# mLSTM layer on one core: stabiliser rows and state weights spread over the partitions by DMA instead of by TensorE

## What is computed

```python
log_d = where(causal, cum_f[t] - cum_f[s] + li[s], -inf)
log_inter = cum_f + m_st
m_t = maximum(log_inter, max(log_d, axis=-1))           # the stabiliser of each row
w_inter = exp(log_inter - m_t)                          # weight of the state in each row
scores = (q k^T) * exp(log_d - m_t)
num = w_inter * (q c_st) + scores v
den = w_inter * (q n_st) + sum(scores)
h = num / maximum(abs(den), exp(-m_t))
c_st = decay * c_st + (w_k k)^T v                       # and n_st, m_st likewise
```

## Time and profile before

| | us |
|---|---|
| median of three runs (2153.97 to 2157.39) | 2154.73 |
| the profiled execution | 2154.42 |
| its span | 2152.8 |
| TensorE busy | 2121.9 |
| VectorE busy | 1425.7 |
| ScalarE busy | 939.2 |
| GpSimd busy | 250.1 |

### The profile page before, as it was taken

One profiled execution on the slowest core, in us unless ns is written; L12 is line 12 of the kernel. 1 busy time (PEld: TensorE's weight loads), 2 busy tenths in 40 slices (PEclk: granted clock), 3 DMA queues, 4 the chain that ended last, 5 costly groups with the idle time before them and its releaser, 6 DMA issues.

```text
span 2152.8 us, 29471 instructions
## 1 busy us (share of the span) xinstructions
PE 2121.9 (99%) x10424; PEld 1762.6 (82%) x10440; DVE 1425.7 (66%) x2274; ACT 939.2 (44%) x1686; POOL 250.1 (12%) x357
## 2 busy tenths in 40 slices
PE   6999999999999999999999999999999999999999
PEld 5888888888888888888878888888888888888887
DVE  8765476787566565679677644767866657556764
ACT  5433674453333333345444347544533333334443
POOL 3211100021001010100121111001110101001000
PEclk9999999999999999999999999999999999999999
DMA  4333373223322334773414334632233232357443
GB/s 148 110 110 113 109 272 121 84 69 106 105 96 97 117 102 150 270 249 118 152 64 142 118 94 147 233 119 89 68 103 109 97 117 96 105 190 250 152 134 107
DMA packets 200288, 281.56 MB, mean 131 GB/s; under 512 B 12912, under 2 KB 131696, under 8 KB 200176
## 3 DMA queue, kind: packets, MB, share of 16 engines
q1 hardware_dynamic: 171696, 183.07, 26.5%
q0 software_dynamic: 28480, 97.02, 12.9%
HBM read 197.73 MB, written 82.31 MB: 130 GB/s over the span
## 4 chain that ended last, share of the span: by engine, by line
PE 94%; DVE 3%; DMA 1%; ACT 1%; issue 1%; POOL 0%; SPq 0%; DVEq 0%; POOLq 0%
PE ps L2247 13%; PE ps L2250 13%; PE ps L2249 13%; PE ps L1971 7%; PE ps L1975 7%; PE ps L1973 7%; PE ps L2295 6%; PE ps L2297 6%; PE ps L2299 6%; PE ps L1884 3%; PE ps L1886 3%; PE ps L1885 3%; PE ps L1891 2%; PE ps L2157 1%; DMA res<-in_x_dram 1%
## 5 line engine op out<-in xcount | busy, mean ns | idle before, releaser
L1722 DVE TENSOR_TENSOR ring<-raw_f,ring 128x512 fp32r<-128x512 f32 x308 | 211.4, 687 | 188.1 <-ACT ring L1148 186.6
L1148 ACT CAST ring<-raw_f 128x512 fp32r<-128x512 f32 x308 | 191.2, 623 | 208.7 <-PE ps L2250 193.2
L2247 PE MATMUL ps<-u_lo,ring 128*128 128x512 f32 x704 | 275.7, 392 | 0.0
L2250 PE MATMUL ps<-u_hi,ring 128*128 128x512 f32 x704 | 274.1, 389 | 0.0
L2249 PE MATMUL ps<-u_hi,ring 128*128 128x512 f32 x704 | 273.9, 389 | 0.0
L2295 PE MATMUL ps<-ring,ring 128*128 128x512 f32 x616 | 240.5, 390 | 2.0 <-DVE ring L1801 1.9
L2299 PE MATMUL ps<-ring,ring 128*128 128x512 f32 x616 | 239.7, 389 | 0.0
L2297 PE MATMUL ps<-ring,ring 128*128 128x512 f32 x616 | 239.7, 389 | 0.0
L2247 PE MATMUL ps<-t_op,ring 128*128 128x512 f32 x528 | 206.0, 390 | 0.0
L2250 PE MATMUL ps<-t_op,ring 128*128 128x512 f32 x528 | 205.5, 389 | 0.0
L2249 PE MATMUL ps<-t_op,ring 128*128 128x512 f32 x528 | 205.4, 389 | 0.0
(11 more groups left out here) (223 smaller groups left out, 4180.3 us busy)
## 6 DMA issues: line engine op xcount, KB each, us to landing
ops_hbm<-kept POOLq DMA_DIRECT2D x154, 256.0 KB, 2.4
g_in<-ops_hbm SPq DMA_DIRECT2D x154, 256.0 KB, 2.7
raw<-in_ml_w_in_dram SPq DMA_DIRECT2D x24, 1024.0 KB, 5.4
proj_hbm<-pkept POOLq DMA_DIRECT2D x96, 256.0 KB, 2.7
raw_f<-in_ffn_w_gate_dram SPq DMA_DIRECT2D x44, 512.0 KB, 4.7
raw_f<-in_ffn_w_up_dram SPq DMA_DIRECT2D x44, 512.0 KB, 4.6
b<-in_ffn_w_down_dram SPq DMA_DIRECT2D x88, 256.0 KB, 4.6
x_in<-in_x_dram SPq DMA_DIRECT2D x16, 512.0 KB, 6.3
```

What stands on the lines that cost most here:

```text
L1148: nc.scalar.copy(four(ring[slot][:, 0, :]), feed_source(q, s)).then_inc(w_hi_done, 1)
L1722: nc.vector.tensor_tensor(four(ring[slot][:, 1, :]), feed_source(q, s), four(ring[slot][:, 0, :].bitcast(F32)), ALU.subtract).then_inc(w_l ...
L2247: pe.matmul(banks(bank), wh, moved(kind, 1, k), start=(fresh and k == 0), stop=False, skip_group_check=True)
L2250: last = pe.matmul(banks(bank), wl, moved(kind, 0, k), start=False, stop=(k == 3), skip_group_check=True)
```

## The change

The rows are spread by DMA. Behind the gates GpSimd stores `t4` and `t2` to a new tensor in DRAM, `rows_hbm` (`store_rows`, behind the stores of projection groups 1 and 4). SP loads them back, for each chunk, with one row on many partitions: `negb` [128, 8 heads, 128] and `wq` [128, 4 pairs, 128], two buffers of each (`load_rows`). VectorE adds the causal mask to `negb` in SBUF (`mask_rows`), ScalarE takes its exponentials from `negb`, and VectorE its weights and the decay from `wq`. `spread`, the products of `weights` (now `turn_keys`, the key transposes alone), `negm`, `wint`, `pick`, `ident_b`, `dec` and their set-up go away. `state_sums` no longer waits for `qw_done` and `dec_done`; `outputs` waits for `qw_done`. `load_res(0)` moves ahead of the last store of the projections. "Orders" are a few moves of `op_hi` and `op_lo` (high and low parts of turned tiles) past neighbouring work on ScalarE and VectorE.

```diff
+                def load_rows(c):
+                    s = c % 2
+                    if c >= 2:
+                        sp.wait_ge(dmat_done, h * 64 + 8 * (c - 1))
+                        sp.wait_ge(qw_done, h * 8 + c - 1)
+                        sp.wait_ge(state_done, h * 32 + 4 * (c - 1))
+                    sp.dma_start(negb[s][:, :, :].rearrange("p i t -> p (i t)"),
+                                 rows_hbm[h, 0, c:c + 1, :].partition_broadcast(P)).then_inc(negb_loaded[s], 16)
+                    for a in range(2):
+                        rows = rows_hbm[h, 1, c, :].rearrange("(g a n) -> a g n", a=2, n=P)
+                        sp.dma_start(wq[s][64 * a:64 * a + 64, :, :], rows[a].partition_broadcast(64))\
+                            .then_inc(wq_loaded[s], 16)
...
                 load_qkc(2)
+                load_rows(2)
                 load_og(1)
                 load_wo(1, 0)
...
                 for c in range(3, TILES):
                     load_qkc(c)
+                    load_rows(c)
                     load_vtc(c)
                     load_og(c)
...
+                                pool.wait_ge(p_fed, h * PU + PU - 1)
+                                load_res(0)
                             pool.wait_ge(o_gated, done + 3 + i)
                             store_block(g, k)
...
+                    if g in (1, 4):
+                        store_rows(0 if g == 1 else 1)
...
-                        nc.scalar.activation(dmat[:, i, :], ps[:, spread_bank(c) + i // 4, (i % 4) * P:(i % 4) * P + P],
-                                             ACT.Exp, bias=colt[:, c, i:i + 1]).then_inc(dmat_done, 1)
+                        nc.scalar.activation(dmat[:, i, :], negb[c % 2][:, i, :], ACT.Exp, bias=colt[:, c, i:i + 1])\
+                            .then_inc(dmat_done, 1)
...
+                def mask_rows(c):
+                    dve.wait_ge(negb_loaded[c % 2], h * 64 + 16 * (c // 2) + 16)
+                    nc.vector.tensor_tensor(negb[c % 2][:, :, :], negb[c % 2][:, :, :],
+                                            mask[:, :].unsqueeze(1).broadcast_to([P, HEADS, P]), ALU.add)\
+                        .then_inc(darg_done, 1)
...
+                    if n == unit_at(PG - 1, 0):
+                        mask_rows(0)
+                    if n == unit_at(PG - 1, 2):
+                        mask_rows(1)
...
-                    nc.vector.tensor_copy(dec[:, :], banks(2).rearrange("p (g t) -> p g t", t=P)[:, :, P - 1])\
-                        .then_inc(dec_done, 1)
-                    nc.vector.tensor_tensor(qw[:, :, :], banks(2).rearrange("p (g t) -> p g t", t=P),
-                                            qkc[c % 2][:, 0:4, :], ALU.mult).then_inc(qw_done, 1)
+                    nc.vector.tensor_tensor(qw[:, :, :], wq[c % 2][:, :, :], qkc[c % 2][:, 0:4, :], ALU.mult)\
+                        .then_inc(qw_done, 1)
...
                         hg_low(c - 1)
+                        if c + 1 < TILES:
+                            mask_rows(c + 1)
                     update_state(c)
...
                     op_hi(0, 2)
+                    op_hi(0, 3)
                     norm1_sum(0, 4)
-                    op_hi(0, 3)
...
+                    op_lo(0, 4)
                     proj_lo(0, 3)
-                    op_lo(0, 4)
...
+                op_lo(st + 1, 5)
                 feed_low(0, 3)
-                op_lo(st + 1, 5)
...
-                        if TURN_AT <= e < TURN_AT + 4:
-                            op_lo(2 * (h + 1), e - TURN_AT)
                         if e in ROWS_AT:
                             norm1_rows(h + 1, ROWS_AT[e])
                         if e in SUMS_AT:
                             sum_early(2 * (h + 1), SUMS_AT[e])
+                        if TURN_AT <= e < TURN_AT + 4:
+                            op_lo(2 * (h + 1), e - TURN_AT)
```

More of the change, by code:

```diff
@@ L723, in _ @@
                 pool.wait_ge(turned, st * OP_UNITS + OP_UNITS)
-                for tile in (cols[:, :], negm[:, :].bitcast(F32), wint[:, :].bitcast(F32)):
-                    nc.gpsimd.memset(tile, 0.0).then_inc(prep_done, 1)
+                nc.gpsimd.memset(cols[:, :], 0.0).then_inc(prep_done, 1)
                 def store_block(g, k):
@@ L888, in gate_part @@
                             .then_inc(gate_act, 1)
-                        nc.scalar.copy(negm[0:HEADS, now], t4[:, :]).then_inc(gate_act, 1)
                     if step == 2:
```

146 lines of the change are left out of this document (57 added, 89 removed).

## The result

The changed kernel takes 2142.88 us (median of 5 runs, 2140.78 to 2145.35), the kernel before 2154.73: 11.85 us less, a ratio of 0.9936 (95% interval 0.9926 to 0.9947). The forecast was 2137.5 with a range from 2126 to 2145, faster by over 0.2%. The sign and the range held; 17.2 us were forecast and 11.85 came. The forecast's own range, 2133 to 2141, was missed: only the part of the range that the second rival had added holds the measured time. The profiled execution took 2141.53 us, its span is 2139.8.

A forecast was written before the change was run, and what follows sets the result against it. TensorE was taken as the bound, except in chunks 0 to 2, where it already waits for VectorE. 13.2 + 1.5 + 0.9 + 1.25 + 0.2 = 17.05 us off 2154.42 gave 2137.4, forecast as 2137.5, range 2126 to 2145.

The forecast's parts named there:

- Rival 2: Chunks 0 to 2: TensorE's new waits lower its granted clock, +2 to +7 us, so 2139.5 to 2144.5; chance 0.17.
- 1.65 us a chunk leave TensorE: All 16 chunks: stabiliser products 1.25 us and state weights 0.40 leave TensorE, 26.4 us in all as the ceiling.
- Chunks 4 to 7 earn all of it: Chunks 4 to 7, both halves: the mask add fits VectorE's wait, so the whole 1.65 us a chunk is earned, -13.2 us.
- Rival 4: Mask add on VectorE takes 3.0 us, not 1.14, where SBUF is busy; no difference, 2151.5 us; chance 0.06.
- rival 3: Mask adds wait for rows spread by DMA; from 16 us a transfer, 12 later chunks lose 2 us each, 2161; chance 0.05.
- The exponentials from SBUF: ScalarE's eight exponentials a chunk read SBUF, not PSUM: 0 to 0.06 us more each, 0.06 taken on the path.
- Chunks 0 to 3: Early chunks, VectorE already full: only 0.75 to 1.5 of their 6.6 us are gained; 0.75 a half taken, -1.5 us.
- What is put in its place: Per chunk: one VectorE mask add of 1.14 us, exponentials from SBUF, three SP transfers; four small GpSimd stores a half.
- The -0.9 for res in the second half: Second half's early chunks: the earlier load removes a wait for res of 1.56 us instead of 0.68, -0.9 us more.
- The orders: Moved splits and sums: -1.25 us between the halves, -0.2 in the feed, 0 at the start.
- Rival 1: Early chunks run with TensorE too, so all 26.4 us are earned, 2126 us; chance 0.15.

The follow-up runs named there:

- transfers in order of need: Changed kernel with only transfers reordered: chunk 2's rows first, vtc ahead of rows and qkc from chunk 3, res a chunk later, gain2 behind chunk 3's rows; 2137.21 us.
- old-orders run: Changed kernel with the operand splits at the start, between the halves and in the feed back in the order of before; 2144.78 us.
- the waits filled: Changed kernel with vtc asked for first from chunk 3 on, and unread matmuls added where TensorE waits for VectorE in chunks 1 and 2; 2139.83 us.
- the last version: Changed kernel with transfers in order of need and both VectorE's and ScalarE's splits of w_out moved later; 2131.19 us, ratio 0.9889.
- the two runs on the mask: Changed kernel with vtc first, 2139.85 us; the same with the mask add of chunks 2 and 3 on one head of eight, 2138.25 us.
- vtc first: Changed kernel with SyncE asking for vtc, then the rows, then qkc from chunk 3 on, where it was qkc, rows, vtc; 2139.85 us.
- moving VectorE's splits: Changed kernel with transfers in order of need and VectorE's splits of w_out moved off its chain to the keys of chunk 2; 2135.90 us.

## Why the prediction was right, point by point

**1.65 us a chunk leave TensorE.** Right, and a little low. From chunk 4 to 7 the period fell from 20.24 to 18.51 us, 1.73. The difference is the 0.1 that I kept back from the state weights' 0.50 for a change of the array's rows; next to nothing of it stayed: 1.25 + 0.50 = 1.75.

**Chunks 4 to 7 earn all of it.** Right. A period of the changed kernel in the windows (length; busy of TensorE, its weight loads, VectorE, ScalarE, GpSimd; clock, DMA share, GB/s), which answers to the earlier trace rows, and VectorE's timeline, which answers to the earlier trace rows:

```profile
352.83:371.34 18.51, 18.51 (x134) 15.54 (x133) 14.09 (x28) 8.60 (x19) 0.56 (x1) 1.00 0.47 157
```

```profile
350.73 1.22 DVE L1544 TENSOR_TENSOR negb<-negb,mask 128x1024 f32<-128x1024 f32 x1
353.03 1.13 DVE L1621 SCALAR_TENSOR_TENSOR state<-state,wq,ps 128x129 f32<-128x129 f32 x4 [1.08 <-PE ps L2154]
```

The mask add takes the 1.22 us of the row it was taken from, VectorE's busy time is 14.09 where 14.2 was worked out, and its wait ahead of the state update 1.08 where 1 was. Rival 4 (a slow add) has nothing for it, and rival 3 is wrong for these chunks: no mask add there stands for its row.

**The exponentials from SBUF.** 128 of them are busy for 39.2 us, 35.0 before, so 0.033 us each; 0.06 was taken from rows of another shape. The estimate of 0.043 that the prediction had made from the Trainium skill ("VectorE: DVE Perf Modes", the section on the TRN2 errata) was nearer, and still above what these rows give.

**Chunks 0 to 3.** Here the prediction failed, in one step. The waits for VectorE came where it put them: in the two halves 1.92 and 1.92 us for the state, 0.63 and 1.81 for pkept, 2.72 and 2.72 for the keys, so 5.3 and 6.5 a half against "some 6". Seven eighths of the mask add cost 0.93 in the full VectorE, and the keys of chunk 2 come 36.27 us behind the turn of v of chunk 0 in the first half, 36.26 before, inside "between 0.3 earlier and 0.5 later":

```profile
308.36 1.10 PE L2135 MATMUL ps<-v,kw 128*64 128x129 f32 x16 [2.72 <-DVE kw L1593]
```

In the second half, where the row is 1.30 late, they come at 37.75 (37.13 before), though the prediction had them 0.4 to 1.2 earlier there. The failed step is in "What is put in its place": "On SP come three transfers a chunk (768 KB in SBUF)" and no price. I priced only the row itself, as rival 3, and that at VectorE; what is queued behind the rows on SyncE, `vtc`, I did not ask, and neither what an earlier `res` is put ahead of. The runs put there what it cost: 4.6 us of wait for `vtc`, 1.3 for the row of chunk 2 in one half (rival 3 had named this: "queued beside the same transfers as gain2, and at 10.1 would already cost 1 us a half"). With the transfers in order of need the stretches are 59.71 and 60.36, where the forecast's terms (0.75, and 0.75 + 0.9) give 60.15 and 60.14, and the time 2137.21, where the forecast was 2137.5; since the kernel before took 2156.89 on that chip, its ratio of 0.9906 is better than the forecast's 0.992, by some 3 us.

**The -0.9 for res in the second half.** Not confirmed. The wait goes in both halves, as forecast, but put back it is only 0.29 in this kernel, and the early load makes the row late instead.

**The orders.** Between the halves 1.1 us (1.9 to 0.8 us of wait for the ring), 1.25 forecast. In the feed no difference (0.9 us of waits at the turn of the operands in both), 0.2 forecast. At the start 0.2 at most at the full clock, 0 forecast; the old-orders run is 1.9 us above the changed kernel, with intervals that overlap.

**The rivals.** Rival 2 was right in what happens, a granted clock of 0.66 to 0.68 behind the new waits, and its time (2139.5 to 2144.5) holds the measured one; but its price was not the clock's. With the waits filled, the clock at 1.00 and `vtc` in time, the median was the same and the stretches 1.05 us shorter, where this rival asked for 2 to 7. That the range holds the measured time is owed to this rival, so the range was right by coincidence. Rival 1 was too bright for this kernel, and yet the waits on which it fell could be had: in the last version the early stretches are 4 to 4.6 us shorter than before, of the 6.6 to 7.0 that leave TensorE there.

What stays open: how much of the 1.6 us between the two runs on the mask is its price, as the clock fell in one half of one of them; what the low stretches of the clock cost in the changed kernel by themselves: between 0 and the 1.05 us of the stretches; and why the row of chunk 2 is late in some halves and not in others of the same kernel.

## What to carry to other kernels

When a change turns work of an engine into transfers, price not only whether the new transfer comes in time, but each load that now stands behind it on its queue and each that shares the DMA engines in that stretch: SyncE's queue read against the time at which every tile is needed is the view for it, and putting transfers in order of need was worth 5.7 us by the medians here, 5.9 by the two stretches. In a stretch where several engines are full, a wait taken away uncovers the next one; moving VectorE's splits gave nothing that the ratio shows, and with ScalarE's moved as well 6.0 us in the two stretches. Here a low clock behind a wait cost only what nothing later covered: fill the wait once, and see whether the time moves.

## What the runs showed of the hardware

The granted clock behind a wait is not a matter of that wait's length alone (1.00 is 2.4 GHz, 0.50 is 1.2; windows between hold both). In the changed kernel it fell to 0.66 behind the wait of 1.92 us that ends at 285.05; with vtc first, the same wait at 286.75 (1.91 us) leaves it at 1.00 from 285 to 295. At the start it stayed at 1.00 behind a wait of 2.13 us in one execution and fell to 0.71 behind the same one in another, and that alone moved chunk 0 by 1.7 us. So single executions of this kernel can differ by 1 to 2 us for a reason that lies in no edit.

The DMA engines gave 372 to 412 GB/s from 295 to 310 us, where they were in use throughout. A 512 KB load asked for there took 11.2 to 14.0 us to land in the first half of the changed kernel, 9.7 to 12.5 in the kernel before, and 3.4 at best elsewhere in the changed one. The issuing queue was held too, 2.21 us for one issue; that a full stretch may reach back into the issuing queue I had not reckoned with.
